# PEER expert stage: when the next block's scores are taken, when spare buffers are first used, where a gated product lies, and how far V sums run behind the dots

## The chip, the cores and the metric

The kernel runs on one core of a Trainium2 chip. The metric is the device time of one execution in microseconds, the median of several runs. The work is one inference step of a two-layer backbone on 128 prompt tokens and 512 sample tokens, width 1024, all in float32.

## What is computed

Each layer has a mixer (attention, a state-space scan and a convolution module side by side, one output projection) and then an expert stage, for the prompt tokens and the sample tokens. The expert stage is where the change lies:

```python
def peer_ffn(h, w_q, sub_keys, u_tab, v_tab):        # per block of 128 tokens
        q = (hb @ w_q).reshape(PEER_BLOCK, PEER_HEADS, 2, PEER_QDIM // 2)
        s = jnp.einsum('thsk,snk->thsn', q, sub_keys).astype(jnp.float32)
        top_s, top_i = lax.top_k(s, PEER_TOPK)
...
        gate = jax.nn.softmax(best_s, axis=-1).astype(hb.dtype)
        act = jax.nn.gelu(jnp.einsum('thkd,td->thk', u_tab[idx], hb), approximate=False)
        return jnp.einsum('thk,thkd->td', gate * act, v_tab[idx])
...
    m = jnp.einsum('bsd,df->bsf', jax.nn.silu(cond), lp['w_ada']) + lp['b_ada']
...
    x = x + g1 * mix
    hff = rmsnorm(x, lp['norm2_g']) * (1 + sc2) + sh2
    x = x + g2 * peer_ffn(hff, lp['peer_wq'], lp['peer_keys'], lp['peer_u'], lp['peer_v'])
```

With 8 heads and 16 experts per head, each token has 128 experts of its own out of 16384, and each expert is one row U and one row V of 1024 numbers.

## The kernel before

**Blocks and slots.** A layer's expert stage is five blocks of 128 tokens: the prompt block (g = 0) and sample blocks b = 0 to 3 (g = 1). They are numbered n = 5 l + 0 for the prompt and 5 l + 1 + b for the samples, so layer 0's last sample block is n = 4. A block has 128 slots, one for each chosen expert of its tokens. For a slot, POOL starts an indirect DMA (L699) that brings each token's U and V row, 8 KB for each of 128 partitions, 1.05 MB, into a buffer. DVE makes the dot product of U with the token's row (L1306), ACT the gelu (L1028), DVE a diagonal matrix of gate times gelu (L1315, `weigh`), and PE multiplies it with V in two halves into an accumulator in PSUM (L747, `add_v`, four matmul passes in the trace). For slots from 84 of the prompt block ACT scales V instead (L1034, L1037) and POOL sums it (L677), in POOL's own instruction order between the gathers. A buffer is free again when its V is summed.

**Buffers.** `slot_buffers` writes out which buffer each slot uses. The ring has RING = 5 buffers. Blocks that run alone also have spares, where the projected queries `qT` of sample blocks lie: block b of the samples uses 5 + min(b + 2, 4), that is 7, 8, 9 and 9 buffers. A spare may be filled when the scores of the block whose queries lie there are taken.

**Scores and choice.** After the projection `pq` (16 tiles, L977 on PE, evacuated by ACT at L1224), PE turns the block's token rows (tiles `ht`, L727) and takes scores against the keys (tiles `ps`, L968); ACT drains them (L1211, L1216); DVE's `choose` picks the top 16 with MAX8 and FIND_INDEX8 (L1669, L1676), one piece every second slot of the block before, and `gates` follows at slot 122. PE runs `score_block(b + 1)`, all six tiles, before its first `add_v` of block b. POOL waits, before slot 0 of sample block b, for the chosen indices of b (`s_idx`) and for the last score tile of block b + 1.

**Work beside.** The prompt block's slots run beside the sample mixer, and layer 0's last sample block (n = 4) beside layer 1's modulation and prompt mixer. Each engine's program has points in the mixer, `beside.point(stage, i)`; the tables BESIDE_SAMPLE and BESIDE_PROMPT say how many steps are taken at each (`mod` 24 points of 2 steps, the output projection `wo` 4 of 2, `pq` 16 of 1, and so on), and `rest()` takes what is left. At step m DVE takes dot m and then `weigh` of m - 1, and PE's `add_beside` takes `add_v` of m - 2. The other sample blocks run alone: three in layer 0, four in layer 1. In an alone block PE's `add_v(n, k)`, DVE's `dot(n, k)`, `weigh(n, k)` and POOL's gathers are plain loops; `add_peer(n - 1)` takes the finished sum of the block before into x at slot 2.

**PSUM.** Rotating tiles are handed out in an order written down by `psum_order`, over the banks that the accumulator leaves; filling one waits until the tile that had the bank has been evacuated.

**Output projection.** For each of 16 sample tiles and 4 prompt tiles in a layer, DVE multiplies the PSUM tile by the gate into an SBUF tile `otmp` (L1653) and adds that to x (L1654), 40 pairs in all.

Of the kernel before, what the change touches and what calls it, by code (L numbers as in the profile page):

```python
# [137 lines left out]
def points(*runs):  # L138
# [6 lines left out]
                       ("head", range(24), 1), ("wo", range(0, 16, 2), 2), ("wo", range(1, 16, 2), 1), ("n2", [7], 3), ("pq", range(16), 1))  # L145
# [7 lines left out]
SECOND_AT, GATES_AT = 30, 122  # L153


def slot_buffers():


    place, before, turn = [], [], []
    used, times = {}, {}  # L160
    for n in range(L * NBLK):
        b = n % NBLK - 1
        alone = b >= 0 and (b < 3 or n // NBLK == L - 1)
        ring = range(RING + (min(b + 2, SPARE) if alone else 0))
        for k in range(SLOTS):
            j = min(ring, key=lambda x: used.get(x, -1))
            place.append(j)
            before.append(used.get(j, -1))
            turn.append(times.get(j, 0) + 1)
            used[j], times[j] = n * SLOTS + k, turn[-1]  # L170
    return place, before, turn
# [87 lines left out]
def psum_order():  # L259

    out = []
    for l in range(L):
        out += [(s, l, 0, i) for s, i, _ in mod_steps()]
        for g in range(2):
# [28 lines left out]
            for b in range(1, nb):  # L293
                out += [("ht", l, g, 2 * b), ("ht", l, g, 2 * b + 1)]
                out += [("ps", l, g, 4 * b + i) for i in range(4)]
# [3 lines left out]
def build(nc, x_in, ckvT_c, kpeT_c, h0, condT, w_ada, b_ada, w_in, w_uq, w_ukv, w_out, w_pq, keysT, uv, par, row, consts,  # L299
# [5 lines left out]
    with ExitStack() as ctx:  # L305
# [357 lines left out]
        def _(pool):  # L663
# [15 lines left out]
            for l in range(L):  # L679
                for g in range(2):  # L680
                    for b in range(GROUP_BLOCKS[g]):
# [24 lines left out]
        def _(pe):  # L706
# [61 lines left out]
            for l in range(L):  # L768
# [17 lines left out]
                for g in range(2):  # L786
# [171 lines left out]
                    def score_block(b, first=0, last=4):  # L958

                        for half in range(0 if first else 2):  # L960
                            t = fill("ht", l, g, 2 * b + half)
                            for c in range(4):
                                ins = turn(t[:, c * P:(c + 1) * P], hT[:, 4 * half + c, b * P:(b + 1) * P])
                            done(ins, "ht")
                        for k in range(first, last):
                            t = fill("ps", l, g, 4 * b + k)
                            for m in range(4):
                                ins = pe.matmul(t[:, m * P:(m + 1) * P], qT[:, b, 4 * k + m, :],  # L968
                                                keys[:, m % 2, :], start=True, stop=True)
                            done(ins, "ps")  # L970

                    for u in range(PQ_UNITS):
# [8 lines left out]
                        if u == 3:  # L981
                            pe.wait_ge(*free["pq"].at(l, g, 7))
                            score_block(0, 0, 2)
                    pe.wait_ge(*free["pq"].at(l, g, 15))
                    score_block(0, 2, 4)
                    beside.rest()
                    if g == 0:
                        beside.start(blk(l, 0, 0), BESIDE_SAMPLE, {})
                        continue
                    for b in range(nb):  # L990
                        if b + 1 < nb:
                            score_block(b + 1)
# [4 lines left out]
                        for k in range(SLOTS):  # L997
                            add_v(n, k)


        @block.scalar
        def _(act):
# [46 lines left out]
            for l in range(L):  # L1049
# [4 lines left out]
                for g in range(2):  # L1054
# [151 lines left out]
                    def drain_scores(b, first=0, last=4):  # L1206
                        for half in range(0 if first else 2):
                            t = tile_of("ht", l, g, 2 * b + half)
                            if b >= 2 and half == 0:
                                act.wait_ge(s_dot, (blk(l, g, b) - 1) * SLOTS)  # L1210
# [648 lines left out]
```

## Time and profile before

| | us |
|---|---|
| median of 3 runs | 4936.78 |
| lowest, highest | 4931.02, 4948.26 |
| profiled execution | 4939.01 |
| its span | 4937.2 |

Over the span PE is busy 3736.8 us (76%), DVE 3339.0 (68%), POOL 1688.4 (34%), ACT 874.1 (18%), at a mean granted clock of 0.917. The gathers' queue takes 68.1% of the DMA engines' time, the mean rate is 303 GB/s. In the page's row of GB/s in 40 slices, the slices of alone blocks stand at 419 to 421, except those with a block boundary, at 361 to 374.

Read it so: busy time says which engine could not be removed, not which is waited for. A row of a timeline has the idle time before the instruction and what ended it in brackets; a row of waits sums such idle time by who waited and for whom; a stretch gives every engine's busy time with the DMA share and rate, which says whether the transfers are full.

### The profile page before, as it was taken

The page shows a single profiled execution, that of the slowest core. Times are in us where ns is not written, and L with a number is a line of the kernel's source. Part 1 is how long each engine was busy: PE and PEld are TensorE (multiplying, and loading weights), DVE is VectorE, ACT ScalarE, POOL GpSimd, SP SyncE. Part 2 cuts the span into 40 slices and gives each one's busy share as a digit, 9 for nine tenths or more (in the row PEclk, how much of TensorE's full clock was granted, in tenths as well). Part 3 has the DMA queues.
Part 4 walks back from the last instruction along what each step waited for, and adds up shares of the span by engine and source line. Part 5 has one row for each costly group of instructions (what it writes and reads, how often), then busy time and mean ns, then how long its engine had stood idle before and what let it go on. Part 6 is the DMA issues. An engine that isn't in the chain of part 4 may idle for free. (4 is left out here: it accounts for less than half of the span.)

```text
span 4937.2 us, 36000 instructions
## 1 busy us (share of the span) xinstructions
PE 3736.8 (76%) x10702; PEld 1850.5 (37%) x10702; DVE 3339.0 (68%) x8175; ACT 874.1 (18%) x2387; POOL 1688.4 (34%) x1374
## 2 busy tenths in 40 slices
PE   7578678767777777788878786785977787777776
PEld 6464334533222222235535443344422232222222
DVE  1546765757887858754564866568588787686666
ACT  0111125431101010010121111353310100100101
POOL 0001111664544434422222011117544354344432
PEclk9789788989999999999989897897999999999999
DMA  8335455766998989999969353557499899899998
GB/s 266 102 117 179 159 184 206 256 211 257 419 420 364 421 364 420 421 389 391 350 237 353 108 206 137 191 204 255 170 374 421 366 421 421 361 421 421 412 421 340
DMA packets 342149, 1497.69 MB, mean 303 GB/s; under 512 B 31425, under 2 KB 176449, under 8 KB 178113
## 3 DMA queue, kind: packets, MB, share of 16 engines
q0 software_dynamic: 184320, 1342.26, 68.1%
q1 hardware_dynamic: 157632, 153.13, 9.6%
q8 instruction: 85, 1.39, 0.1%
q14 instruction: 112, 0.91, 0.1%
HBM read 1491.97 MB, written 3.31 MB: 303 GB/s over the span
## 5 line engine op out<-in xcount | busy, mean ns | idle before, releaser
L747 PE MATMUL expert_acc<-uv_ring,diag 128*128 128x512 f32 x3392 | 1704.9, 636 | 398.2 <-DVE diag L1315 389.0
L699 POOL DMA_INDIRECT uv_ring<-uv,expert_index x936 | 1081.8, 1156 | 2489.3 <-PE expert_acc L747 1938.4
L747 PEld LDWEIGHTS expert_acc<-uv_ring,diag 128*128 128x128 f32 x3392 | 624.3, 199 | 1389.7 <-DVE diag L1315 860.3
L1306 DVE CUSTOM_DVE_ANT_0 uv_ring<-uv_ring,arena 128x1024 f32<-128x1024 f32 x680 | 831.9, 1223 | 237.6 <-DMA uv_ring<-uv,expert_index 234.7
L747 PE MATMUL expert_acc<-arena,diag 128*128 128x512 f32 x1376 | 684.3, 629 | 261.8 <-DVE diag L1315 193.5
L1028 ACT ACTIVATE gelu<-u_dot 128x1 f32<-128x1 f32 x1280 | 258.5, 203 | 2912.3 <-DVE u_dot L1306 2911.7
L1315 DVE TENSOR_SCALAR diag<-const_mats,expert_gate,gelu 128x128 f32<-128x128 f32 x1192 | 433.2, 363 | 258.6 <-ACT gelu L1028 163.2
L699 POOL DMA_INDIRECT arena<-uv,expert_index x344 | 392.8, 1142 | 588.0 <-PE expert_acc L747 461.4
L1306 DVE CUSTOM_DVE_ANT_0 arena<-arena 128x1024 f32<-128x1024 f32 x344 | 421.0, 1224 | 172.1 <-DMA arena<-uv,expert_index 170.8
L747 PEld LDWEIGHTS expert_acc<-arena,diag 128*128 128x128 f32 x1376 | 241.9, 194 | 693.6 <-DVE diag L1315 421.3
L1306 DVE CUSTOM_DVE_ANT_0 uv_ring<-uv_ring,prompt_rows 128x1024 f32<-128x1024 f32 x256 | 357.5, 1401 | 128.0 <-DMA uv_ring<-uv,expert_index 99.7
L727 PE MATMUL rotating<-const_mats,arena 128*128 128x128 f32 (+1 forms) x622 | 124.6, 334 | 330.1 <-ACT arena L1022 141.4
L977 PE MATMUL rotating<-hT,w_ring 128*128 128x128 f32 (+1 forms) x1024 | 289.4, 444 | 17.7 <-DVE hT L1293 12.9
L677 POOL TENSOR_TENSOR arena<-uv_ring,arena 128x1024 f32<-128x1024 f32 x88 | 211.6, 2405 | 128.7 <-ACT uv_ring L1037 127.4
L727 PEld LDWEIGHTS rotating<-const_mats,arena 128*128 128x128 f32 (+1 forms) x622 | 90.7, 169 | 403.2 <-ACT arena L1022 146.7
L977 PEld LDWEIGHTS rotating<-hT,w_ring 128*128 128x128 f32 x1024 | 162.6, 198 | 149.2 <-issue 129.8
L810 PE MATMUL rotating<-hT,w_ring 128*128 128x512 f32 (+1 forms) x640 | 181.8, 440 | 0.1
L950 PE MATMUL rotating<-w_ring,hT 128*128 128x256 f32 x640 | 147.1, 391 | 13.9 <-DVE x L1654 12.0
L776 PE MATMUL rotating<-w_ring,hT 128*128 128x256 f32 x528 | 126.4, 395 | 33.6 <-DMA w_ring<-w_ada 29.5
L1676 DVE FIND_INDEX8 arena<-arena 128x8 uint32<-128x128 f32 (+1 forms) x480 | 148.9, 330 | 0.0
L1669 DVE MAX8 arena<-arena 128x8 f32<-128x128 f32 (+1 forms) x480 | 123.6, 323 | 37.5 <-ACT arena L1216 37.1
L815 PE MATMUL rotating<-w_ring,hT 128*128 128x256 f32 (+1 forms) x640 | 137.9, 378 | 12.9 <-DVE hT L1293 12.9
(208 smaller groups left out, 3146.5 us busy)
## 6 DMA issues: line engine op xcount, KB each, us to landing
w_ring<-w_ada SPq DMA_DIRECT2D x66, 512.0 KB
w_ring<-w_in SPq DMA_DIRECT2D x64, 512.0 KB
w_ring<-w_pq SPq DMA_DIRECT2D x64, 512.0 KB
w_ring<-w_out SPq DMA_DIRECT2D x32, 512.0 KB
uv_ring<-w_ada SPq DMA_DIRECT2D x30, 512.0 KB, 5.0
uv_ring<-uv,expert_index POOLq DMA_INDIRECT x936
arena<-b_ada SPq DMA_DIRECT2D x48, 128.0 KB
arena<-uv,expert_index POOLq DMA_INDIRECT x344
```

What stands on the lines that cost most here:

```text
L677: nc.gpsimd.tensor_tensor(pool_sum(n), UV[SLOT_AT[m]][:, D:2 * D], pool_sum(n), ALU.add).then_inc(s_pa, 1)
L699: pool.indirect_dma_start(out=UV[j], out_offset=None, in_=uv, in_offset=bass.IndirectOffsetOnAxis(ap=idxs[:, n % 2, k:k + 1], axis=0)).the ...
L727: return pe.transpose(out, src, C[:, C_ID, :])
L747: ins = pe.matmul(acc[:, half, :], diag[:, TURN[m] % DIAGS, :], UV[SLOT_AT[m]][:, D + 512 * half:D + 512 * half + 512], start=(k == 0), st ...
L810: ins = pe.matmul(t[:, 0:T], w[:, c, (i % 2) * P:(i % 2 + 1) * P], hT[:, c, 0:T], start=(c == 0), stop=(c == DC - 1))
L815: ins = pe.matmul(t[:, 0:width], hT[:, c, b * P:(b + 1) * P], w[:, c, 0:width], start=(c == 0), stop=(c == DC - 1))
L950: ins = pe.matmul(t[:, 0:WU], hT[:, c, b * P:(b + 1) * P], w[:, c, :], start=(c == 0), stop=(c == DC - 1))
L977: ins = pe.matmul(t[:, 0:T], w[:, c, k * P:(k + 1) * P], hT[:, c, 0:T], start=(c == 0), stop=(c == DC - 1))
L1028: nc.scalar.activation(gel[:, m % DOTS:m % DOTS + 1], dots[:, m % DOTS:m % DOTS + 1], ACT.Gelu).then_inc(s_gel, 1)
L1306: V_.tensor_tensor_reduce(UV[j][:, 0:D], UV[j][:, 0:D], rows_of(n), 1.0, 0.0, ALU.mult, ALU.add, dots[:, m % DOTS:m % DOTS + 1]).then_inc( ...
L1315: V_.tensor_scalar(diag[:, TURN[m] % DIAGS, :], C[:, C_ID, :], gat[:, n % 2, k:k + 1], gel[:, m % DOTS:m % DOTS + 1], ALU.mult, ALU.mult). ...
L1676: ins = V_.max_index(dst[:, r, at_], val[:, r, at_], src(r))
```

## The change

1. POOL no longer waits for the next block's scores at slot 0. It waits for the score tile that frees a spare's place right before that spare's first use. `slot_buffers` orders buffers by `since`, so that in block 0 the first spare comes at slot 6 and the second at slot 8, and blocks 1 and 2 begin with their new spare.
2. PE takes block 1's scores before block 0's loop. In block b it turns block b + 1's rows at slots 8 and 9 and takes block b + 2's scores at slots 100 to 103. ACT drains the rows at slots 8 and 9 and the scores at slots 124 to 127. `psum_order` follows. DVE waits for the turned rows at slot 0 of their block.
3. In BESIDE_SAMPLE `pq` has two steps at each of its first eight points, instead of one at each of 16.
4. The gated product of the output projection is written in place in the PSUM tile.
5. `add_beside` takes `add_v` of m - 1 instead of m - 2 in block n = 4. Prompt blocks keep m - 2.

```diff
-                       ("head", range(24), 1), ("wo", range(0, 16, 2), 2), ("wo", range(1, 16, 2), 1), ("n2", [7], 3), ("pq", range(16), 1))
+                       ("head", range(24), 1), ("wo", range(0, 16, 2), 2), ("wo", range(1, 16, 2), 1), ("n2", [7], 3), ("pq", range(8), 2))
...
+ROWS_AT, SCORES_AT, DRAIN_AT = 8, 100, 124
+
+def turned_at(g, b, k, scores_at):
+    nb = GROUP_BLOCKS[g]
+    if b + 1 < nb and ROWS_AT <= k < ROWS_AT + 2:
+        return ("ht", b + 1, k - ROWS_AT)
+    if b + 2 < nb and scores_at <= k < scores_at + 4:
+        return ("ps", b + 2, k - scores_at)
+    return None
...
+        if b == 0:
+            since.update({RING: n * SLOTS, RING + 1: n * SLOTS + 1})
+        elif alone and b < 3:
+            since[RING + b + 1] = -1
         ring = range(RING + (min(b + 2, SPARE) if alone else 0))
         for k in range(SLOTS):
-            j = min(ring, key=lambda x: used.get(x, -1))
+            j = min(ring, key=lambda x: since.get(x, -1))
...
+                            if g and j >= RING and j not in SLOT_AT[blk(l, 1, 0) * SLOTS:m]:
+                                pool.wait_ge(*full["ps"].at(l, 1, 4 * (j - RING) + 3))
...
                             if k == 0:
                                 pool.wait_ge(*s_idx.at(l, g, 2 * b))
-                                if g:
-                                    pool.wait_ge(*full["ps"].at(l, 1, min(4 * b + 7, 15)))
...
             def add_beside(n, m):
-                if 2 <= m <= SLOTS + 1 and not by_pool(n, m - 2):
-                    add_v(n, m - 2)
+                k = m - (1 if n % NBLK else 2)
+                if 0 <= k < SLOTS and not by_pool(n, k):
+                    add_v(n, k)
...
-                    for b in range(nb):
-                        if b + 1 < nb:
-                            score_block(b + 1)
+                    for k in range(4):
+                        score(1, k)
+                    for b in range(nb):
...
                         for k in range(SLOTS):
                             add_v(n, k)
+                            turned = turned_at(g, b, k, SCORES_AT)
+                            if turned is not None:
+                                (turn_rows if turned[0] == "ht" else score)(*turned[1:])
...
-                        if 0 < b < nb - 1:
-                            drain_scores(b + 1)
...
+                            turned = turned_at(g, b, k, DRAIN_AT)
+                            if turned is not None:
+                                (drain_rows if turned[0] == "ht" else drain_scores)(*turned[1:])
...
-                        chain(V_.tensor_tensor(otmp[i % 2], t[:, 0:WU], G[:, gate_tile(l, 0, g), u * WU:(u + 1) * WU], ALU.mult))
-                        V_.tensor_tensor(x, x, otmp[i % 2], ALU.add).then_inc(free["wo"].sem, 1)
+                        chain(V_.tensor_tensor(t[:, 0:WU], t[:, 0:WU], G[:, gate_tile(l, 0, g), u * WU:(u + 1) * WU], ALU.mult))
+                        V_.tensor_tensor(x, x, t[:, 0:WU], ALU.add).then_inc(free["wo"].sem, 1)
...
-                        dve.wait_ge(*free["ht"].at(l, g, 2 * b + 1))
+                        if b == 0:
+                            dve.wait_ge(*free["ht"].at(l, g, 1))
                         if b + 1 == nb and l + 1 < L:
                             add_peer(n - 1)
+                            dve.wait_ge(*free["ht"].at(l, g, 2 * b + 1))
                             beside.start(n, BESIDE_PROMPT)
                             continue
...
                         for k in range(SLOTS):
+                            if b and k == 0:
+                                dve.wait_ge(*free["ht"].at(l, g, 2 * b + 1))
                             dot(n, k)
```

## Rows read from the trace of the kernel before

**Rows 1.** Stretches of the span: busy us of each engine, granted clock, DMA share, GB/s.
```profile
1200.00:1450.00 250.00, 191.03 (x392) 67.89 (x391) 216.94 (x562) 25.62 (x107) 119.80 (x99) 0.99 1.01 417
...
1800.00:1850.00 50.00, 32.44 (x96) 14.45 (x94) 23.28 (x50) 9.28 (x24) 14.15 (x15) 0.89 0.70 279
...
2190.00:2375.00 185.00, 163.85 (x567) 102.39 (x566) 83.68 (x191) 8.92 (x44) 51.68 (x44) 1.00 1.03 385
2375.00:2730.00 355.00, 280.47 (x1054) 166.81 (x1052) 203.66 (x535) 68.79 (x193) 84.77 (x79) 0.91 0.83 302
```

**Rows 2.** Timeline of POOL at the two kinds of boundary: start, duration, work, [idle before <-releaser].
```profile
1839.74 0.94 POOL L699 DMA_INDIRECT arena<-uv,expert_index  x1 [24.71 <-PE rotating L968]
...
4606.91 0.94 POOL L699 DMA_INDIRECT uv_ring<-uv,expert_index  x1 [11.72 <-issue]
```

**Rows 3.** Timeline of DVE: the first dot of four sample blocks.
```profile
1170.81 1.22 DVE L1306 CUSTOM_DVE_ANT_0 arena<-arena 128x1024 f32<-128x1024 f32 x1 [7.34 <-DMA arena<-uv,expert_index]
...
1508.58 1.23 DVE L1306 CUSTOM_DVE_ANT_0 arena<-arena 128x1024 f32<-128x1024 f32 x1 [13.16 <-DMA arena<-uv,expert_index]
...
4268.44 1.23 DVE L1306 CUSTOM_DVE_ANT_0 arena<-arena 128x1024 f32<-128x1024 f32 x1 [13.43 <-DMA arena<-uv,expert_index]
...
4592.45 1.22 DVE L1306 CUSTOM_DVE_ANT_0 uv_ring<-uv_ring,arena 128x1024 f32<-128x1024 f32 x1 [0.52 <-DMA uv_ring<-uv,expert_index]
```

**Rows 4.** Timeline of POOL: the prompt block's sums (L677) and the first gather after.
```profile
1042.30 2.36 POOL L677 TENSOR_TENSOR arena<-uv_ring,arena 128x1024 f32<-128x1024 f32 x1
...
1058.34 2.36 POOL L677 TENSOR_TENSOR arena<-uv_ring,arena 128x1024 f32<-128x1024 f32 x1 [0.25 <-ACT uv_ring L1037]
...
1165.10 0.95 POOL L699 DMA_INDIRECT arena<-uv,expert_index  x1 [8.84 <-PE rotating L968]
```

**Rows 5.** Timeline of ACT: evacuations of two pq tiles, layer 0.
```profile
1083.46 0.60 ACT L1224 ACTIVATE arena<-rotating 128x512 f32<-128x512 f32 x1 [4.67 <-PE rotating L977]
...
1090.33 0.60 ACT L1224 ACTIVATE arena<-rotating 128x512 f32<-128x512 f32 x1 [4.67 <-PE rotating L977]
```

**Rows 6.** Groups of 913 to 1013, the sample mixer's output projection: busy us, mean ns.
```profile
L677 POOL TENSOR_TENSOR arena<-uv_ring,arena 128x1024 f32<-128x1024 f32 x23 | 55.3, 2404 | 0.6
...
L1654 DVE TENSOR_TENSOR x<-x,arena 128x256 f32<-128x256 f32 x15 | 40.8, 2720 | 0.5
```

**Rows 7.** Two lines' instructions over the span: ns min/median/max, first and last start.
```profile
L1653 DVE TENSOR_TENSOR arena<-rotating,gates x40: 410/414/426, 256.1 to 3424.6; 128x256 f32<-128x256 f32 x40
...
L1654 DVE TENSOR_TENSOR x<-x,arena x40: 425/2184/3135, 256.6 to 3425.0; 128x256 f32<-128x256 f32 x40
```

**Rows 8.** Timelines of PE and DVE in layer 1's modulation, beside block 4.
```profile
2195.08 3.62 PE L776 MATMUL rotating<-w_ring,hT 128*128 128x256 f32 x16
2198.53 1.88 PE L747 MATMUL expert_acc<-uv_ring,diag 128*128 128x512 f32 x4
2200.61 1.98 PE L747 MATMUL expert_acc<-uv_ring,diag 128*128 128x512 f32 x4 [0.20 <-DVE diag L1315]
...
2202.65 3.62 PE L776 MATMUL rotating<-w_ring,hT 128*128 128x256 f32 x16
...
2259.18 1.98 PE L747 MATMUL expert_acc<-uv_ring,diag 128*128 128x512 f32 x4 [1.63 <-DVE diag L1315]
...
2191.50 1.22 DVE L1306 CUSTOM_DVE_ANT_0 uv_ring<-uv_ring,arena 128x1024 f32<-128x1024 f32 x1
...
2201.99 1.23 DVE L1306 CUSTOM_DVE_ANT_0 uv_ring<-uv_ring,arena 128x1024 f32<-128x1024 f32 x1 [1.44 <-DMA uv_ring<-uv,expert_index]
...
2376.84 1.23 DVE L1306 CUSTOM_DVE_ANT_0 uv_ring<-uv_ring,arena 128x1024 f32<-128x1024 f32 x1
```

**Rows 9.** Timeline of PE beside block 4, in layer 1's prompt pq.
```profile
2668.48 1.88 PE L747 MATMUL expert_acc<-uv_ring,diag 128*128 128x512 f32 x4
2670.20 1.95 PE L977 MATMUL rotating<-hT,w_ring 128*128 128x128 f32 x16
```

**Rows 10.** Waits in 2375 to 2730: us in total, times, longest.
```profile
DVE uv_ring L1306 <- DMA uv_ring<-uv,expert_index: 79.1, 40, 5.6
```

More of the change, by code:

```diff
@@ L292, in psum_order @@
             out += [("pq", l, g, i) for i in range(8, 16)] + [("ps", l, g, 2), ("ps", l, g, 3)]
-            for b in range(1, nb):
-                out += [("ht", l, g, 2 * b), ("ht", l, g, 2 * b + 1)]
-                out += [("ps", l, g, 4 * b + i) for i in range(4)]
+            if g:
+                out += [("ps", l, g, 4 + i) for i in range(4)]
+                for x in (turned_at(g, b, k, SCORES_AT) for b in range(nb) for k in range(SLOTS)):
+                    if x is not None:
+                        out.append((x[0], l, g, (2 if x[0] == "ht" else 4) * x[1] + x[2]))
     return out
@@ L957, in _, with turn_rows, score @@
                     pe.wait_ge(*free["n2"].at(l, g, 2 * nb - 1))
[L958 to L970, printed above, removed]
+                    def turn_rows(b, half):
+                        t = fill("ht", l, g, 2 * b + half)
+                        for c in range(4):
+                            ins = turn(t[:, c * P:(c + 1) * P], hT[:, 4 * half + c, b * P:(b + 1) * P])
+                        done(ins, "ht")
+                    def score(b, k):
+                        t = fill("ps", l, g, 4 * b + k)
+                        for m in range(4):
+                            ins = pe.matmul(t[:, m * P:(m + 1) * P], qT[:, b, 4 * k + m, :],
+                                            keys[:, m % 2, :], start=True, stop=True)
+                        done(ins, "ps")
                     for u in range(PQ_UNITS):
@@ L982, in _ @@
                             pe.wait_ge(*free["pq"].at(l, g, 7))
-                            score_block(0, 0, 2)
+                            for half in range(2):
+                                turn_rows(0, half)
+                            for k in range(2):
+                                score(0, k)
                     pe.wait_ge(*free["pq"].at(l, g, 15))
-                    score_block(0, 2, 4)
+                    for k in range(2, 4):
+                        score(0, k)
                     beside.rest()
@@ L1205, in _, with drain_rows, drain_scores @@
                     act.wait_ge(*free["n2"].at(l, g, 2 * nb - 1))
[L1206 to L1210, printed above, removed]
[L1211 to L1216 removed]
+                    def drain_rows(b, half):
+                        t = tile_of("ht", l, g, 2 * b + half)
+                        if b >= 2 and half == 0:
+                            act.wait_ge(s_dot, (blk(l, g, b) - 1) * SLOTS)
+                        nc.scalar.activation((htok[b % 2] if g else htok_p[:])[:, 512 * half:512 * half + 512], t, ACT.Copy).then_inc(free["ht"].sem, 1)
+                    def drain_scores(b, k):
+                        t = tile_of("ps", l, g, 4 * b + k)
+                        if b and k == 0:
+                            act.wait_ge(*s_idx.at(l, g, 2 * b - 1))
+                        nc.scalar.activation(scs[:, 4 * k:4 * k + 4, :].rearrange("p s n -> p (s n)"), t, ACT.Copy).then_inc(free["ps"].sem, 1)
                     def gate_exp(i, heads=slice(0, PH), l=l, g=g):
@@ L1226, in _ @@
                         if i == 7:
-                            drain_scores(0, 0, 2)
-                    drain_scores(0, 2, 4)
+                            for half in range(2):
+                                drain_rows(0, half)
+                            for k in range(2):
+                                drain_scores(0, k)
+                    for k in range(2, 4):
+                        drain_scores(0, k)
                     beside.rest()
@@ L1244, in _ @@
                                 gate_exp(1, slice(HALF, PH))
-                                drain_scores(1)
+                                for i in range(4):
+                                    drain_scores(1, i)
                             if b + 1 < nb and k == GATES_AT:
```

10 lines of the change are left out of this document (3 added, 7 removed).

## The prediction, made before the changed kernel ran

> **What bounds the kernel now.** I read the stretches first. Where a sample block runs alone, the DMA engines are full: 417 GB/s at a share of 1.01, with DVE busy 217 us and PE 191 us of 250 [rows 1]. POOL then issues a gather each 2.49 us, so a block of 128 slots can't take less than 128 x 2.49 = 318.7 us. No edit of PE, DVE or ACT work changes that; only time in which the gathers stop can be won. The reader is to see where the rate falls: 279 GB/s in the 50 us around the boundary between two alone blocks, 302 GB/s in 2375 to 2730, where layer 0's last sample block runs beside layer 1's prompt mixer [rows 1]. The timeline of POOL gives the reason at the boundary: the block's first gather goes out at 1839.74, after 24.71 us idle that ended with L968, the score matmuls of the block after [rows 2]. There are four such boundaries (into sample blocks 1 and 2 of each layer); the three not shown have 21.82, 22.23 and 24.50. First dot to first dot gives the price: 1508.58 - 1170.81 = 337.8 us for a block that ends so, and 4592.45 - 4268.44 = 324.0 for the one whose successor isn't followed by scoring [rows 3]. The four intervals are 337.8, 336.7, 338.3 and 336.6, so 19.1, 18.0, 19.6 and 17.9 above 318.7.
>
> The median of 4936.8 is 2.2 under the profiled execution (4939.0); the sum is made against 4939.0 and the difference carried over. A measurement of this kernel tells about 0.3%, 15 us, from no change.
>
> **Boundaries (spares at first use, scores at slot 100).** POOL's wait at slot 0 for the next block's scores goes. Then PE still has to pass the last slot's V, DVE its last dot, and `add_peer` comes at slot 2. The boundary without scoring shows what is late next: POOL still pauses 11.72 us [rows 2], yet the first dot comes after only 0.52 us of idle time [rows 3], and the excess is 324.0 - 318.7 = 5.3. So the floor is 5.3 left of each: -(13.8 + 12.7 + 14.3 + 12.6) = -53. But those boundaries have 9 buffers, the four here have 7 and 8 (a spare fewer is 2.49 us less of gathers in flight), and DVE is busy 217 of 250 us while it chooses the next block's experts [rows 1], so it catches up slowly. I leave 8 us instead of 5.3 on each: 53 - 4 x 2.7 = 42.4, A = **-43**, bounds -53 and -30. The turned rows move to slots 8 and 9 and the score tiles to 100 to 103 on PE (about 0.5 us a tile, against PE idle 59 of 250 us), ACT's drains to 8, 9 and 124 to 127 (0.6 us each, like the 128x512 copy of [rows 5], ACT busy 26 of 250): nothing, by that cover. DVE's wait for the turned rows at slot 0 finds them there since slot 9. If that cover is gone, four slots with a drain before their gelu each add 0.6 us at most, 2.4 us per boundary; that is inside the bounds.
>
> **Start of the first sample block.** After POOL's last sum for the prompt block the first gather goes out at 1165.10, 8.84 us later, on L968 [rows 4]. Layer 1 has 9.36. Without that wait the chosen indices and the free buffers are there already: -8.6 per layer. PE scores block 1 before its first V, 4 tiles, which the first gathers' flight (1170.81 - 1165.10 = 5.7 us, [rows 3, 4]) covers.
>
> **Projection pq, 8 x 2 points instead of 16 x 1.** The same 16 steps move under the first eight pq tiles, spaced 1090.33 - 1083.46 = 6.87 us [rows 5]. Two slots then have 6.87, 3.43 each; POOL at full speed needs (1058.34 - 1042.30)/4 = 4.01 [rows 4]. Over eight points that is 8 x 2 x 0.58 = 9.2 us late, of which the queue that ACT and DVE have ahead takes some 3: ACT evacuates tile 7 about 6 us late, PE, with four accumulators to rotate through, starts the later ones late by the same, and afterwards the spacing has no beside work to give it back. Gain -8.6, loss +5.7: B = **-3 per layer, -6**; bounds -17 (no loss) and +4 (all 9.2 lost and 1 more).
>
> **Gated product in PSUM.** L1654 adds two SBUF operands: 0.43 us alone, median 2.18, up to 3.14 beside POOL's sum [rows 7], and 2.72 on average in the sample mixer's output projection [rows 6]. With the product left in PSUM the add has one SBUF operand, as L1653 has, and L1653 takes 0.41 to 0.43 in all 40 instances, beside the same POOL [rows 7]. So DVE gains 40 x 1.66 = 66 us. But there the stage is POOL's: L677 is busy 55.3 us for 23 sums in 100 us [rows 6] and gathers fill the rest, 100/23 = 4.35 us per slot against 4.01 in the next stage [rows 4]. The 0.34 is what POOL loses to DVE: 24 slots x 0.34 = 8 per layer. I take 7: C = **-14**; bounds 0 (POOL has another reason for 4.35) and -30 (PE's and DVE's own waits come free too).
> The Trainium skill has a rule for this, in "SBUF — State Buffer", section "Who interferes with whom": a DVE operation with both inputs in SBUF and a GpSimd operation that reads SBUF lock one another out for a whole instruction. The rows agree: L1654 at 2.72 us stands beside POOL's sums, L1653 with one SBUF input stays at 0.41.
> Against the edit stands "Perfetto Trace Analysis", section "Optimizing Scalar/DVE Operations": DVE's access overhead is about 125 ns in PSUM and 60 in SBUF. By that, as an estimate, 40 pairs x 2 accesses x 65 ns = +5 us of DVE work; no run here shows it yet.
>
> **V one step behind the dots (block n=4).** At a point of two steps DVE does dot(m), diag(m-1), dot(m+1), diag(m). PE today adds m-2, whose diagonal is long there, at once after its modulation tile, and then m-1 after 0.20 us [rows 8]. After the change it adds m-1 and m: neither diagonal exists when the tile ends, so both adds follow the diagonals. So today the first add fills the time in which DVE works (evacuation, dot, diagonal), and after the change PE is idle in that time and both adds come behind it. One add is four matmul passes, 1.72 us: the next work starts that long after one begun at 2668.48 [rows 9]. Behind PE's wait stands the next modulation tile, and behind that DVE's evacuation. The unit is 7.57 us (2195.08 to 2202.65, [rows 8]) and becomes 9.29; a gate unit, where PE waits 1.63 instead of 0.20 [rows 8] and turns no tile (0.22 less), goes from 7.57 + 1.43 - 0.22 = 8.78 to 10.50. From dot 2 (2191.50) to dot 46 (2376.84) there are 14 plain and 8 gate intervals in 185.3 us [rows 8]: 14 x 9.29 + 8 x 10.50 = 214.1, so +28.8. The first add at modulation tile 0 waits for its diagonal too, +3. The output projection's four tiles have two steps each: 4 x 1.72 = +7. The other many-step points (n1, st, v, n2): +4. In pq there is one step per tile and PE is the pace, with no wait for a diagonal [rows 9]: nothing.
> Against it: buffer k is summed one point sooner, so gather k+5 starts sooner. DVE waited 79.1 us for gathers in 2375 to 2730 [rows 10], but the loop gather k+5, sum k, diag k, dot k+1 stays as it is, and the transfer share is 0.83 on average [rows 1] because it is full while weights are loaded. I give back 11. Together 28.8 + 3 + 7 + 4 - 11 = **+32**; bounds +5 and +48.
>
> **Sum.** -43 - 6 - 14 + 32 = -31: 4939.0 - 31 = 4908 for a profiled execution, **4906** for the median.
>
> **Rivals.**
> 1. *The earlier sums pay* (0.22). If most of the 79 us of DMA waits come from gathers issued too late, not from full queues, D is -15 instead of +32. For: POOL is busy only 85 of 355 us there, and 302 GB/s is far from 417 [rows 1]. Against: PE would have to be idle when the diagonal comes, and in the modulation it is busy 164 of 185 us [rows 1]. Then -43 - 6 - 14 - 15 = -78: 4859.
> 2. *The boundary stall only moves* (0.12). With DVE at 217 of 250 [rows 1] and 7 or 8 buffers, the first dot is late by the last dot, `add_peer` and the flight, and only half of 53 comes: A = -20, total -8: 4929.
> 3. *Slower: the adds' wait is DVE's whole chain* (0.08). Each modulation point waits for its second gather too, whose lateness today (1.44 us, [rows 8]) hides behind PE's tile: 24 x 1.44 = +34 on top of +32. With A at -30 and pq's full loss on both layers (B = +4) and C = -14: -30 + 4 - 14 + 66 = +26: 4963. It decides from the point where D passes 43 + 6 + 14 = 63.
> 4. *The edit in PSUM does nothing* (0.12), POOL's 4.35 being its own: C = 0, 4920.
> My own forecast has the rest, 0.46, within 4890 to 4922.
>
> The range leaves out rival 3 and the lower half of rival 1: **4854 to 4936**. Faster by over 0.3% (under 4922): 0.46 + 0.22 + most of 4 and a little of 2, 0.79. Within: 0.14. Slower (over 4951.6): 0.07.
>
> **What would show it.** Right: no POOL pause over 14 us at the four boundaries and intervals of first dots of 324 to 329; the first gather after the prompt's last sum within 1 us; L1654 at about 0.45 us in all 40; modulation units of 9.3 us beside block 4, with PE's first add waiting about 2 us on diag L1315; pq tile 7 late by some 6 us. Wrong: modulation units under 8 us (rival 1), with DVE's DMA waits well under 79; intervals still above 332 (rival 2); units over 10.5 us (rival 3).

## The result, and the profile after

The changed kernel takes 4982.9 us (median of 5 runs, 4971.0 to 4988.6), the kernel before 4941.3 (4931.0 to 4948.3, 5 runs): a ratio of 1.0082, interval 1.0061 to 1.0102. It is 42 us slower. The forecast was 4906, within 4854 to 4936: wrong side and out of the range. The profiled execution of the kernel after is 4982.9, its span 4981.1.

From the page of the kernel after, the rows of busy time, PE clock and rate in 40 slices:

```profile
PE 3788.9 (76%) x10702; PEld 1875.8 (38%) x10702; DVE 3322.9 (67%) x8175; ACT 871.5 (17%) x2387; POOL 1692.3 (34%) x1374
...
PEclk9788788879999999998888997888899999999999
...
GB/s 265 99 116 177 156 184 201 259 233 233 420 416 414 421 411 421 421 330 296 301 226 284 189 183 149 184 206 262 226 249 418 415 415 421 414 421 421 401 421 344
```

PE is busy 52 us more than the 3736.8 of before for the same 10702 instructions, which is the first sign that they ran slower, and slices 18 to 20 (some 2120 to 2490 us) stand at 330, 296 and 301 GB/s. The four slices with a boundary between two alone blocks are at 411 to 415, where before they were at 361 to 366.

Where the 44 us between the two profiled spans lie is read from the timelines of DVE, as the time from the first dot of a block to the first dot of the next:

| stretch | before | after | difference | the prediction's term |
|---|---|---|---|---|
| layer 0 prompt block | 777.0 | 785.5 | +8.5 | B, C |
| block n=1 (boundary into 2) | 337.8 | 326.8 | -11.0 | A |
| n=2 | 339.7 | 329.1 | -10.6 | A |
| n=3 | 337.4 | 336.2 | -1.2 | - |
| **n=4, beside layer 1's mixer** | 624.2 | 708.7 | **+84.5** | D = +32 |
| layer 1 prompt block | 783.8 | 781.0 | -2.8 | B, C |
| n=6 | 338.3 | 328.3 | -10.0 | A |
| n=7 | 336.6 | 324.0 | -12.6 | A |
| n=8, 9 | same | same | 0 | - |

(The prediction gave n=2 as 336.7; read again it is 339.7.) Added up with -0.9 us ahead of and behind them, these are the 44. The four boundaries give -44.2, the forecast -43. The loss is in block 4, but for the +8.5 of layer 0's prompt block.

One of the four boundaries, into layer 0's sample block 2, in the rows of stretches of the kernel after; the row of before is in [rows 1], with 279 GB/s:

```profile
1810.00:1860.00 50.00, 36.15 (x73) 14.12 (x74) 37.97 (x99) 8.57 (x27) 22.52 (x19) 0.90 0.99 400
```

POOL's timeline in the same place has no pause like the 24.71 us of [rows 2] ahead of the block's first dot. One of 10.41 us comes some 3 us after it:

```profile
1827.42 1.54 POOL L718 DMA_INDIRECT uv_ring<-uv,expert_index  x1 [2.36 <-PE expert_acc L766]
...
1847.47 0.94 POOL L718 DMA_INDIRECT arena<-uv,expert_index  x1 [10.41 <-PE expert_acc L766]
```

It waits for PE to free a buffer, and PE waits 7.57 us for `add_peer` at slot 2, which takes the finished sum out of the accumulator (L1364):

```profile
1843.42 6.05 PE L766 MATMUL expert_acc<-arena,diag 128*128 128x512 f32 x8 [7.57 <-DVE x L1364]
```

The other three boundaries have the same pause, 9.72, 10.56 and 10.24 us. This is what is left of the stop. On DVE, where before the first dot came at 1848.30:

```profile
1834.49 1.23 DVE L1342 CUSTOM_DVE_ANT_0 arena<-arena 128x1024 f32<-128x1024 f32 x1 [0.68 <-DMA arena<-uv,expert_index]
```

The first dot waits 0.68 us for its gather.

L1690 is the line that was L1654, the add of the gated product. The row of before is in [rows 7], 425/2184/3135 ns; its instructions over the span are now:

```profile
L1690 DVE TENSOR_TENSOR x<-x,rotating x40: 420/421/422, 255.9 to 3493.2; 128x256 f32<-128x256 f32 x40
```

Now block 4 under the modulation, from dot 2 to dot 46. The columns are those of [rows 1]: PE clock and DMA share stand ahead of the last number. First the kernel before:

```profile
2191.50:2376.80 185.30, 164.11 (x564) 101.72 (x562) 85.01 (x195) 8.92 (x44) 51.68 (x44) 1.00 1.03 385
```

And after:

```profile
2182.40:2427.50 245.10, 191.47 (x560) 112.32 (x560) 84.49 (x195) 8.93 (x44) 41.21 (x44) 0.86 0.87 294
```

The same 22 intervals, 185.3 us before, are 245.1 us. The granted clock is 0.86 instead of 1.00, and the transfers run at 294 GB/s instead of 385: they are no longer the limit, they wait. The timeline of PE shows two plain units, where [rows 8] has 7.57 us for one:

```profile
2197.03 3.62 PE L796 MATMUL rotating<-w_ring,hT 128*128 128x256 f32 x16
2202.57 5.40 PE L766 MATMUL expert_acc<-uv_ring,diag 128*128 128x512 f32 x8 [1.92 <-DVE diag L1351]
2207.80 0.38 PE L746 MATMUL rotating<-const_mats,arena 128*128 128x128 f32 x2
2208.02 3.62 PE L796 MATMUL rotating<-w_ring,hT 128*128 128x256 f32 x16
2213.56 3.70 PE L766 MATMUL expert_acc<-uv_ring,diag 128*128 128x512 f32 x8 [1.92 <-DVE diag L1351]
2217.09 0.38 PE L746 MATMUL rotating<-const_mats,arena 128*128 128x128 f32 x2
2217.31 3.62 PE L796 MATMUL rotating<-w_ring,hT 128*128 128x256 f32 x16
```

The unit is as forecast: PE waits 1.92 us for the diagonal, then both adds come. But eight passes of the adds take 3.70 us in one unit (eight at 0.43, the 2.4 GHz level) and 5.40 in the other, where four of them run at 0.86 (1.2 GHz). So units alternate between 9.29 and 10.99 us. Under the gate tiles PE waits 3.35 us and nearly all eight passes are slow, and a unit is 13.4 us:

```profile
2262.10 3.62 PE L796 MATMUL rotating<-w_ring,hT 128*128 128x256 f32 x16
2269.06 6.57 PE L766 MATMUL expert_acc<-uv_ring,diag 128*128 128x512 f32 x8 [3.35 <-DVE diag L1351]
2275.46 3.62 PE L796 MATMUL rotating<-w_ring,hT 128*128 128x256 f32 x16
2282.43 6.71 PE L766 MATMUL expert_acc<-uv_ring,diag 128*128 128x512 f32 x8 [3.35 <-DVE diag L1351]
```

### The profile page after: what moved, and what is told of

Its sections match the earlier page's. It is cut to its first block, busy times and chain, and to the rows that moved or that the text cites. A ratio compares the mean times of both kernels' runs of the same rounds, so it can differ in the third digit from the quotient of the medians.

```text
span 4981.1 us, 35992 instructions
## 1 busy us (share of the span) xinstructions
PE 3788.9 (76%) x10702; PEld 1875.8 (38%) x10702; DVE 3322.9 (67%) x8175; ACT 871.5 (17%) x2387; POOL 1692.3 (34%) x1374
## 4 chain that ended last, share of the span: by engine, by line
PE 34%; DMA 28%; DVE 24%; POOL 5%; issue 5%; ACT 4%; SPq 1%; DVEq 0%; POOLq 0%; ACTq 0%
DMA uv_ring<-uv,expert_index 22%; PE expert_acc L766 16%; DVE uv_ring L1342 6%; DMA arena<-uv,expert_index 4%; PE rotating L796 3%; PE rotating L998 3%; POOL arena L696 3%; PE rotating L830 2%; DVE diag L1351 2%; POOL uv_ring L718 2%; PE rotating L835 2%; DVE arena L1342 1%; DVE arena L1499 1%; DVE arena L1712 1%; PE rotating L746 1%
## 5 line engine op out<-in xcount | busy, mean ns | idle before, releaser
L766 PE MATMUL expert_acc<-uv_ring,diag 128*128 128x512 f32 x3408 | 1767.6, 653 | 496.0 <-DVE diag L1351 487.6
L766 PEld LDWEIGHTS expert_acc<-uv_ring,diag 128*128 128x128 f32 x3408 | 645.8, 205 | 1513.6 <-DVE diag L1351 932.5
L1342 DVE CUSTOM_DVE_ANT_0 uv_ring<-uv_ring,prompt_rows 128x1024 f32<-128x1024 f32 x256 | 411.2, 1611 | 182.0 <-DMA uv_ring<-uv,expert_index 143.3
L970 PEld LDWEIGHTS rotating<-w_ring,hT 128*128 128x128 f32 x640 | 123.8, 194 | 28.7 <-DVE x L1690 6.3
```

What stands on the lines that cost most here:

```text
L766: ins = pe.matmul(acc[:, half, :], diag[:, TURN[m] % DIAGS, :], UV[SLOT_AT[m]][:, D + 512 * half:D + 512 * half + 512], start=(k == 0), st ...
L970: ins = pe.matmul(t[:, 0:WU], hT[:, c, b * P:(b + 1) * P], w[:, c, :], start=(c == 0), stop=(c == DC - 1))
L1342: V_.tensor_tensor_reduce(UV[j][:, 0:D], UV[j][:, 0:D], rows_of(n), 1.0, 0.0, ALU.mult, ALU.add, dots[:, m % DOTS:m % DOTS + 1]).then_inc( ...
```

## The experiments

Eleven kernels ran. "Two behind" means `add_beside` as in the kernel before. All ratios are against the kernel before. For each the stretch of block 4 up to dot 46 and after it is read as in the table above.

**1. Two steps behind again.**

```diff
-                k = m - (1 if n % NBLK else 2)
+                k = m - 2
```


> The changed kernel with add_beside back at m - 2 for block 4 too; all else as changed. Theory A (the step one behind alone costs the +84.6 us that block 4 grew by, first dot to first dot 709 us instead of 624): time about 4983 - 85 = 4898, 0.991 of the kernel before, block 4 at 624 again and the granted clock in its modulation at 1.00. Theory B (part of the growth is the new order of the spares and scores before block 4, the step itself within its bound of 48): time at 4935 or more, block 4 at 660 or more.


Measured: 4881.6 us (4880.4 to 4884.1), ratio 0.988 (0.987 to 0.990). So this one line costs 4982.9 - 4881.6 = 101 us, and the rest of the change gains 58. Block 4 is 610.8 us, 97.9 less than in the changed kernel: 7.2 from dot 0 to 2, 61.0 (184.0 against 245.1) to dot 46, and 29.7 after. Theory A holds; block 4 even ends 13.4 below the kernel before, which it didn't expect. It is the shortest of the six kernels whose sums in block 4 are all two behind: the others have 616.8 to 624.2, and the three all one behind with no full-array filler 708.7 to 712.6. By these the step costs 85 to 102 us in block 4.

**2. One step behind, and nothing else of the change.**

```diff
-                if 2 <= m <= SLOTS + 1 and not by_pool(n, m - 2):
-                    add_v(n, m - 2)
+                k = m - (1 if n % NBLK else 2)
+                if 0 <= k < SLOTS and not by_pool(n, k):
+                    add_v(n, k)
```


> The kernel before with add_beside at m - 1 for block 4 and nothing else. Theory A: +85 us, about 5026, ratio 1.017; in the modulation half of the units at 9.3 us and half at 11.0, gate units at 13.5, granted clock about 0.86. Theory B: at most +48, ratio 1.010 or less, all units at 9.3 and 10.5 with the clock at 1.00.


Measured: 5032.9 us (5026.3 to 5045.2), ratio 1.0194 (1.0178 to 1.0210), +93 us. Block 4 is 712.6 us. The loss doesn't depend on the other parts.

**3. PE kept busy with one row of the array.** Does the clock fall because PE stands idle ahead of the adds? The added matmuls take a row of a constant that is all zeros, so the sums stay as they are.

```diff
+                if n % NBLK and 1 <= k < 48 and m % 2 == 0:
+                    for half in range(2):
+                        pe.matmul(acc[:, half, :], C[0:1, C_LS, :], C[0:1, 0:4, :], start=False, stop=False, skip_group_check=True)
```


> The changed kernel, and in block 4's slots under the modulation PE runs two more matmuls of zeros (four passes, 1.72 us) ahead of the first add of each point, into the accumulator, so that it works in the time in which it would wait for the diagonal. Theory C (of the 66 us that the modulation stretch grew by, what lies over the predicted 32 is a lower granted clock after PE's idle time): clock near 1.00, plain units all at about 9.3, gate units at 10.5 to 11, stretch shorter by 25 to 35 us, time about 4950. Theory D (the excess is the loop of gather, dot, diagonal, sum): units stay at 9.3 and 11.0 or grow by the added 1.72 us, time 4983 or more.


Measured: 4980.9 us (4975.2 to 4988.3), ratio 1.0083. Nothing changed, as theory D has it, though PE has no gap left in a plain unit. Its timeline (L782 are the added passes):

```profile
2213.92 1.98 PE L782 MATMUL expert_acc<-const_mats 1*128 1x512 f32 x4
2215.90 5.40 PE L766 MATMUL expert_acc<-uv_ring,diag 128*128 128x512 f32 x8
2221.14 0.38 PE L746 MATMUL rotating<-const_mats,arena 128*128 128x128 f32 x2
2221.36 3.62 PE L799 MATMUL rotating<-w_ring,hT 128*128 128x256 f32 x16
2224.91 1.98 PE L782 MATMUL expert_acc<-const_mats 1*128 1x512 f32 x4
2226.89 3.70 PE L766 MATMUL expert_acc<-uv_ring,diag 128*128 128x512 f32 x8
```

Its stretch:

```profile
2182.00:2425.00 243.00, 232.81 (x646) 126.10 (x645) 83.06 (x191) 8.92 (x44) 40.26 (x43) 0.86 0.86 292
```

PE is busy 233 of 243 us and the clock is 0.86. The 1-row passes themselves run at 0.43 us and the adds behind them still at 0.86 in every other unit. So an idle PE is not what the low clock needs. This doesn't yet decide against the clock as the cause of the loss, since the added matmuls use one row of the array's 128; the next kernel uses all of them.

**4. The same with all 128 rows.** Weights are a column of zeros spread out, so nothing is added; eight passes in gate units.

```diff
+                if n % NBLK and 1 <= k < 48 and m % 2 == 0:
+                    for half in range(2 * (2 if (m // 8) in (2, 5) else 1)):
+                        pe.matmul(acc[:, half % 2, :], C[:, C_LS, P - 1:P].broadcast_to([P, P]), C[:, 0:4, :], start=False, stop=False, skip_group_check=True)
```


> Like the first filler kernel, but the added matmuls of zero weights use all 128 rows (the first used one row of 128, its passes ran at 0.43 us and the adds behind them still at 0.86), four passes in a plain unit and eight in a gate unit. Theory C (the granted clock falls for want of work on the full array): clock in the modulation above 0.95, adds at 0.43 us a pass, plain units 9.3 us, gate units 10.5 to 11, stretch 257 down to 225, time about 4950. Theory G (it falls with the adds' place behind the diagonals whatever PE does before them): clock 0.86 again and 4980.


Measured: 4952.0 us (4939.6 to 4958.7), ratio 1.0022 (1.0009 to 1.0035): 31 us less than the changed kernel, by adding work. Plain units on PE:

```profile
2203.50 3.62 PE L799 MATMUL rotating<-w_ring,hT 128*128 128x256 f32 x16
2206.96 1.88 PE L782 MATMUL expert_acc<-const_mats 128*128 128x512 f32 x4
2209.04 3.70 PE L766 MATMUL expert_acc<-uv_ring,diag 128*128 128x512 f32 x8 [0.20 <-DVE diag L1354]
2212.58 0.38 PE L746 MATMUL rotating<-const_mats,arena 128*128 128x128 f32 x2
2212.80 3.62 PE L799 MATMUL rotating<-w_ring,hT 128*128 128x256 f32 x16
```

A gate unit:

```profile
2261.91 3.62 PE L799 MATMUL rotating<-w_ring,hT 128*128 128x256 f32 x16
2265.36 3.60 PE L782 MATMUL expert_acc<-const_mats 128*128 128x512 f32 x8
2268.87 3.70 PE L766 MATMUL expert_acc<-uv_ring,diag 128*128 128x512 f32 x8
2272.41 3.62 PE L799 MATMUL rotating<-w_ring,hT 128*128 128x256 f32 x16
```

And the stretch:

```profile
2182.00:2412.00 230.00, 223.30 (x710) 129.63 (x709) 95.84 (x234) 11.92 (x51) 44.62 (x48) 0.99 0.93 326
```

The clock is 0.99, the plain unit is 9.30 us and the gate unit 10.50. Theory C holds. From dot 2 to dot 46 it is 214.5 us; the prediction's sum of the order alone was 214.1. So 185.3 to 214.5 is the order (+29.2), and 214.5 to 245.1 the clock (+30.6).

**5 and 6. One behind in the modulation alone, and after it alone.**

```diff
-                k = m - (1 if n % NBLK else 2)
+                todo = [m - 1] if m < 48 else [] if m == 48 else [m - 2]
```

is the rule for block 4 in the first (cut down: `add_v` is run for each slot of `todo`), and in the second (cut down likewise)

```diff
-                k = m - (1 if n % NBLK else 2)
+                todo = [m - 2] if m < 48 else [46, 47] if m == 48 else [m - 1]
```


> The changed kernel with block 4's sums one step behind up to slot 46 (layer 1's modulation) and two behind after it. If the two stretches add up (modulation 257 against 189 us, the rest 452 against 422), 4881.6 + 68 = 4950. If the rest's +30 is a follow-up of the late modulation, 4980.


Measured: 4956.3 us (4942.1 to 4965.4), ratio 1.0031 (1.0016 to 1.0046); +75 over two behind.


> The changed kernel with block 4's sums two behind under the modulation (up to slot 47) and one behind after it: the other half of the run that was one behind in the modulation alone. If the two halves add up, the stretch from slot 46 to the block's end is 452 us and the modulation 189: 4881.6 + 27 to 30 = 4909 to 4912, below the kernel before. If the loss after the modulation needs the late modulation in front, 4882.


Measured: 4915.8 us (4905.7 to 4917.4), ratio 0.993 (0.991 to 0.995); +34 over two behind. The halves give 75 + 34 = 109 against 101 together: they add up, within what such medians tell. (The medians of the kernel before differ too, 4945.2 us beside experiments 6, 7 and 9, 4940.9 beside 5, and 4939.8 beside 1; with these taken off the halves give 73.6 + 28.8 = 102.) The part after the modulation is a loss too. By stages, experiment 1 against the changed kernel, in us from dot to dot: cT 10.6 to 15.1, the state scan (st) 34.4 to 41.7, yT and v 19.7 to 22.4, attention heads 37.7 to 48.5, output projection 32.0 to 40.8, pq with the rest 152.4 to 154.9; n1, the input projections, taps and n2 are 0.4 to 2.6 shorter. Each column is one profile, and experiment 1 has the shortest scan of all: over the seven kernels two behind in this part and the five one behind, the means are 10.8 and 14.6 for cT, 37.0 and 41.9 for st, 20.3 and 22.1 for yT and v, 38.1 and 46.1 for the heads, 32.3 and 40.8 for the output projection.

**7. Three steps behind.**

```diff
-                k = m - (1 if n % NBLK else 2)
+                k = m - (3 if n % NBLK else 2)
```


> The changed kernel with block 4's sums three steps behind. PE then finds both diagonals ready at each modulation point; its wait of 0.20 us goes, in gate units 1.63, so 10 to 20 us less if PE's waits are all that counts: 4865 to 4870. If the buffers, freed a step later, starve the dots (ring of 5, transfers at a share of 1.0 in the modulation already): DVE's waits for gathers rise above the 75 us of two behind and the time is 4890 or more.


Measured: 4909.6 us (4907.6 to 4917.4), ratio 0.993 (0.991 to 0.995), 28 over two behind (22 by the ratios to the kernel before). The modulation is 183.0 us against 184.0, not 10 to 20 less: the transfers are full there with either lag (a share of 1.04 with two, 1.03 with three), so PE's waits of 0.20 and 1.63 us had cost little. The rest is 455.9 against 422.2. The waits after the modulation, from dot 46 to dot 127, say why; columns are us in total, times, longest. One behind (the changed kernel):

```profile
PE expert_acc L766 <- DVE diag L1351: 65.1, 31, 3.7
...
DVE uv_ring L1342 <- DMA uv_ring<-uv,expert_index: 48.3, 25, 6.9
```

Two behind:

```profile
DVE uv_ring L1342 <- DMA uv_ring<-uv,expert_index: 74.8, 37, 5.5
...
PE expert_acc L766 <- DVE diag L1351: 26.9, 24, 3.1
```

Three behind:

```profile
DVE uv_ring L1342 <- DMA uv_ring<-uv,expert_index: 118.0, 50, 6.9
...
PE expert_acc L766 <- DVE diag L1351: 18.3, 16, 2.7
```

DVE waits 48, 75 and 118 us for gathers, PE 65, 27 and 18 us for diagonals. Going from two steps to one takes 27 us from DVE's waits and adds 38 to PE's; going to three takes 9 from PE's and adds 43 to DVE's.

**8. The gated product in PSUM alone** (the two lines of the change at L1653 and L1654, on the kernel before).


> The kernel before with the gated product written in place in PSUM and nothing else. By the prediction's term C: -14 us, ratio 0.997. By the rival that POOL paces the stage anyway: 0 us, ratio 1.000, although L1654 falls to about 0.45 us in all 40 instances. If DVE's slower access to PSUM counts: up to +5.


Measured: 4928.2 us (4925.5 to 4937.6, 11 runs), ratio 0.9973 (0.9963 to 0.9983), -12.6 us. L1654 is 420/421/422 ns. The stage that the term was about gives less than that. From slot 84 to 108 of the prompt block, beside the sample mixer's output projection, it is 120.5 and 121.1 us in the two layers, before 123.4 and 124.1: -5.9 together. POOL's sums there come each 4.25 and 4.24 us, before each 4.37 and 4.41, not 4.01. POOL's sum is as long as it was, 2.36 us, while many of the gathers between the sums are shorter. Before:

```profile
932.62 1.99 POOL L699 DMA_INDIRECT uv_ring<-uv,expert_index  x1 [0.27 <-POOL arena L677]
```

And with the product in PSUM:

```profile
935.59 1.64 POOL L699 DMA_INDIRECT uv_ring<-uv,expert_index  x1 [0.27 <-POOL arena L677]
```

The profiled execution is 10.8 us shorter than that of the kernel before. The rest lies where the edit does nothing: block 4 has -4.3, none of it at its slots beside an output projection, and slots 16 to 32 of the prompt blocks have +2.9 and -5.3. These stretches differ by as much between kernels that have the same code there: block 4 has 611 to 624 us, slots 16 to 32 in layer 1 107 to 115.

**9. The boundaries alone** (parts 1 and 2 of the change: sums two behind, pq 16 times one, `otmp` as before).


> The kernel before with parts 1 and 2 alone (spares at first use, turned rows at slots 8 and 9, scores at slot 100): sums two behind, pq 16 points of one, gated product in SBUF. Four boundaries shortened by 10 to 13 us each (A = -43 predicted, -52 by the first dots of the changed kernel) and each layer's first gather 4 to 9 us earlier: 4941 - 52 - 12 = 4877. If the parts compete (the gate's 13 us in the same waits), 4885 or more.


Measured: 4881.1 us (4871.1 to 4886.7), ratio 0.987 (0.984 to 0.989). Its four boundary blocks are 43.0 us shorter than before; from slot 96 of the prompt block to the first sample dot it is 207.2 us against 211.9, and 206.9 against 214.5 in layer 1, another 12.3. Block 4 gives 7.4 more, unexplained. The -52 of the expectation was misread: the first dots of the changed kernel give -44.2, as in the table above.

**10. pq back at 16 points of one step**, with sums two behind.

```diff
-                       ("head", range(24), 1), ("wo", range(0, 16, 2), 2), ("wo", range(1, 16, 2), 1), ("n2", [7], 3), ("pq", range(8), 2))
+                       ("head", range(24), 1), ("wo", range(0, 16, 2), 2), ("wo", range(1, 16, 2), 1), ("n2", [7], 3), ("pq", range(16), 1))
```


> As the first kernel, with pq back at 16 points of one step. The trace of the changed kernel has the last pq tile evacuated 14.8 us later than before at 1163.66 (8.9 with the offset of 5.9 from earlier taken off), and slot 127 still in rest(). Theory E (doubling the steps holds ACT's evacuations and costs PE 6 to 9 us per layer): 12 to 18 us faster than with 8 points of two, about 4884, first gather of block 1 about 8.6 us earlier against the last pq tile than before. Theory F (the doubling is hidden by what ends later anyway): within 4 us of it.


Measured: 4874.0 us (4864.4 to 4880.2), ratio 0.986 (0.984 to 0.988), 7.6 under experiment 1. From slot 96 of the prompt block to the first sample dot it is 207.6 and 207.3 us, with 8 points of two 216.8 and 215.9: 17.8 in both layers together. Theory E has the mechanism, and the time lies between the two forecasts. Most of the other 10 are in block 4, 623.2 us here against 610.8; why block 4 differs by 12 us between two kernels with the same program there isn't settled. (The kernel before has 624.2, the run of 9 616.8.) The trace of the changed kernel shows the mechanism. ACT evacuates tile 7 late, PE waits for it, and its clock is down when it goes on (eight turned passes in 1.97 us, 1.09 in the kernel before):

```profile
1063.64 34.50 PE L998 MATMUL rotating<-hT,w_ring 128*128 128x512 f32 x80
1104.27 1.97 PE L746 MATMUL rotating<-const_mats,hT 128*128 128x128 f32 x8 [6.14 <-ACT arena L1254]
```

POOL in the same kernel:

```profile
1168.73 2.37 POOL L696 TENSOR_TENSOR arena<-uv_ring,arena 128x1024 f32<-128x1024 f32 x1 [50.94 <-ACT uv_ring L1065]
1171.22 0.95 POOL L718 DMA_INDIRECT uv_ring<-uv,expert_index  x1
```

POOL's last sum of the prompt block, slot 127's, comes after 50.94 us without work, since slot 127 is in `rest()` behind all 16 tiles, which now end late.

**11. 12 points of one, 4 of two**, sums two behind.

```diff
-                       ("head", range(24), 1), ("wo", range(0, 16, 2), 2), ("wo", range(1, 16, 2), 1), ("n2", [7], 3), ("pq", range(8), 2))
+                       ("head", range(24), 1), ("wo", range(0, 16, 2), 2), ("wo", range(1, 16, 2), 1), ("n2", [7], 3), ("pq", range(12), 1), ("pq", range(12, 16), 2))
```


> Two steps behind, and pq with 12 points of one step and 4 of two, so that the last dots of the prompt block no longer wait in rest() behind the last tile. If POOL's last sum then follows the last tile by one slot instead of two or more: 3 to 8 us per layer faster than with 16 points of one (4874), about 4864. If ACT's evacuations are held as with 8 points of two: 4874 to 4882.


Measured: 4854.3 us (4848.8 to 4858.8), ratio 0.982 (0.980 to 0.984), 87 us under the kernel before, 20 under experiment 10, and the fastest here. That is below both forecasts. Nothing is left for `rest()`; POOL's last sum and first gather are at

```profile
1148.56 2.35 POOL L696 TENSOR_TENSOR arena<-uv_ring,arena 128x1024 f32<-128x1024 f32 x1 [3.32 <-ACT uv_ring L1065]
1151.06 0.95 POOL L718 DMA_INDIRECT uv_ring<-uv,expert_index  x1
```

14 us earlier than the 1165.10 of [rows 4]. From slot 96 to the first sample dot it is 196.6 and 197.2 us.

## Why the prediction was wrong, point by point

**What bounds the kernel** stood: full transfers in the alone blocks at 2.49 us a slot, and the stops between them.

**A, boundaries: -43 forecast, -44.2 in the changed kernel and -43.0 alone.** Leaving 8 us of excess instead of 5.3 was right: they are 8.1, 10.4, 9.6 and 5.3, 8.4 on average, and what is left is PE's wait for `add_peer`, which the term had named. (With 339.7 for n=2 the excess before was 21.0 there, not 18.0, and the sum had 3 us more to win.) Rival 2 is out.

**B, start of the first sample block and pq: -6 forecast.** From slot 96 to the first sample dot the changed kernel has +2.1 and -4.5, so -2; the seven kernels with this code have -2 to +6, +3 on average. The parts were both mis-sized: the start gives 12.3 (17.2 forecast), and the doubled points cost 17.8 over two layers from experiment 10 to 1, 15 on the average of the seven (11.4 forecast). The 5.7 was ACT's hold alone; PE's wait of 6.14 us (0.69 in the kernel before) is about that, and the slow passes behind it came on top. The +8.5 of the table is mostly neither: slots 16 to 32 of layer 0's prompt block take 108 to 111 us in the three kernels with the gated product in SBUF and 112 to 115 in the ten with it in PSUM, far from that code. The cause stays open.

**C, gated product: -14 forecast, -12.6 measured alone, and the match is in good part luck.** The term was POOL's pace going from 4.35 to 4.01 us a slot; it went from 4.37 and 4.41 to 4.25 and 4.24, which is worth 5.9 us in the stage and not 14. Rival 4 (POOL's 4.35 us being its own) is right for more than half of the 0.34: DVE's adds had only lengthened part of the gathers between the sums. The remaining 6 to 7 us of the -12.6 lie elsewhere, with no cause shown. The +5 us estimated from the Trainium skill's "Perfetto Trace Analysis", section "Optimizing Scalar/DVE Operations", isn't there: the add with a PSUM operand takes 0.421 us, the one of two SBUF operands 0.425 at its shortest, and the product takes 0.422 written to PSUM (median of L1689) and 0.414 to SBUF.

**D, one step behind: +32 forecast, bounds +5 and +48, measured +93 alone and +101 within the change.** This is the step that failed: the sum kept 1.72 us for an add at every point, took PE's clock behind its new waits as unchanged, and left out most of the points with two steps after the modulation. Its parts:
- *The units' order*, +28.8 forecast, +29.2 with the clock held up (experiment 4). Right. (The units of [rows 8] add up to 14 x 7.57 + 8 x 8.78 = 176.2 us, 9 short of the 185.3: with transfers at a share of 1.03 PE's order wasn't the whole of the pace before, and the sum did well to start from the 185.3.)
- *The clock*, not in the sum: +30.6 in the modulation. I kept 1.72 us for one add before and after, though I had written that PE would stand idle in each unit. In the kernel before PE is busy 164 of 185 us and the granted clock is 1.00; gaps of 0.20 and 1.63 us leave it there. With gaps of 1.92 us it is down in every other unit, with 3.35 us in each. The Trainium skill has a rule that bears on this in "TensorE: Matmul & The Clock Gate", Part 1, "What's actually happening": the slow state is the default and activity releases it. The rows with idle gaps agree; experiment 3 adds that a PE which the profile shows busy 233 of 243 us isn't enough. The page would have suggested a rival that I didn't write.
- *The first point*: +3 forecast, +5.9 measured (5.85 to 11.77 us from dot 0 to dot 2). PE waits 3.77 us there and its four passes take 3.75.
- *Output projection*: +7 forecast, +8.8.
- *The other points with several steps*: +4 forecast; +25 by the stages of experiment 1 and the changed kernel, +18 by the means. The six head points have two steps each, as the four of the output projection, and 6 x 1.72 = 10.3 was missing; they cost 10.8 (8.1 by the means). The scan's two points of three and cT's of two cost 7.3 and 4.5 (4.9 and 3.7).
- *Gathers a step earlier*: -11 forecast. DVE's waits for gathers did fall, from 74.8 to 48.3 us, more than I gave. But PE's waits for diagonals rose by 38 at the same time, and of the 27 us only -0.4 to -2.6 in each of a few stages is seen in the time. Rival 1 had the mechanism right and its worth wrong.
- Rival 3 was the right side (D over 63 decides) by another mechanism: the units are not 10.5 us for a late second gather but 9.3 and 11.0, in turn, by the clock, and 4963 was still too low.

## What to carry to other kernels

An operation that is moved ahead of its operand on an in-order engine can cost twice on TensorE, as it did here (+29 and +31 us in one stretch): once for the work that no longer hides the wait, and again for the matmuls that run at half clock after it. Cost every point of a hand-written schedule at which several steps are taken, by the tables, before the sum is closed. A lag between producer and consumer had its optimum in between: with one step PE waited, with three the buffers (a ring of 5) came free too late, so try both neighbours of the lag and nothing else with it. And a total that comes out as forecast doesn't show its mechanism: read the stage that the term was about, as in experiment 8.

## What the runs showed of the hardware

- TensorE's granted clock fell with an idle gap of 1.92 us in each plain unit (half of them had four passes at 0.86 us) and of 3.35 us in each gate unit, 0.86 on average over the stretch. It stayed at 1.00 with gaps of 0.20 and 1.63 us.
- Keeping PE busy didn't hold the clock by itself. Passes on one row of 128, in the same gap, left it at 0.86 with PE busy 233 of 243 us; passes on all 128 rows, of zeros, held it at 0.99 and made the kernel 31 us faster.
- A DVE `tensor_tensor` (128x256) with one operand in PSUM took 0.420 to 0.422 us in all 40 cases, most of them beside POOL's sums, where one of two SBUF operands took up to 3.14 us. POOL's own sums stayed at 2.36 us, and many of its gathers between them went from 1.98 to 1.65.
